# Hybrid decoder layer on one core: token rows scaled, halved and turned by transposing DMAs instead of loaded turned and scaled by a spread product

## The reference, cut to what matters

```python
h = rmsnorm(x, norm_g)                     # x / sqrt(mean(x^2) + 1e-6) * norm_g, per token
proj = h @ w_in                            # 1024 -> 3072
# stick-breaking attention (8 heads), RG-LRU, cross-attention into 256 memory tokens,
# each times silu of its gate
out = x + concat(sb_out, lru_out, xa_out) @ w_out
```

## Time and profile before

| | |
|---|---|
| median of three runs | 1594.46 us |
| profiled execution | 1595.76 us |
| its span | 1594.0 us |
| granted TensorE clock, mean | 0.99 of full |
| TensorE busy | 1530.7 us |
| VectorE busy | 1066.6 us |
| ScalarE busy | 882.1 us |
| POOL busy | 313.2 us |
| DMA, mean | 126 GB/s |

### The profile page before, as it was taken

The page is one execution under the profiler, slowest core; times in us unless marked ns, Lnnn a source line. Parts: engine busy times, 40 slices in busy tenths (PEclk is TensorE's granted clock), DMA queues, the critical chain, the costliest instruction groups (busy, mean ns, idle before and its releaser), DMA issues.

```text
span 1594.0 us, 29935 instructions
## 1 busy us (share of the span) xinstructions
PE 1530.7 (96%) x10886; PEld 748.6 (47%) x10886; DVE 1066.6 (67%) x1932; ACT 882.1 (55%) x1593; POOL 313.2 (20%) x305
## 2 busy tenths in 40 slices
PE   4889999999999999999999999999999999999976
PEld 1344444444444444444444444444444444444432
DVE  5889666676666667666666666666766666676662
ACT  5887455565445556544556644555654455565450
POOL 2122111222211222221222221112222112221100
PEclk9999999999999999999999999999999999999987
DMA  9355554544545454554545454544445454545443
GB/s 366 142 155 117 131 125 108 125 121 120 135 102 139 105 128 109 128 132 109 121 122 123 109 130 120 123 111 122 120 119 133 103 140 102 128 112 126 113 90 93
DMA packets 368711, 201.62 MB, mean 126 GB/s; under 512 B 333792, under 2 KB 334240, under 8 KB 367520
## 3 DMA queue, kind: packets, MB, share of 16 engines
q1 hardware_dynamic: 368384, 200.98, 49.4%
q10 hardware_dynamic: 288, 0.13, 0.0%
HBM read 70.73 MB, written 50.53 MB: 76 GB/s over the span
## 4 chain that ended last, share of the span: by engine, by line
PE 69%; ACT 14%; issue 6%; DVE 3%; SPq 0%; DMA 0%; ACTq 0%; POOL 0%; POOLq 0%; DVEq 0%
PE bank L1654 21%; PE bank L1656 21%; PE bank L1655 21%; ACT fail_and_take L936 2%; PE bank L1698 2%; ACT L929 1%; ACT spare L957 1%; ACT L947 1%; ACT L971 1%; ACT L975 1%; PE bank L1799 1%; ACT fail_and_take L826 1%; PE bank L1820 1%; PE bank L1707 1%; DVE spare L1448 1%
## 5 line engine op out<-in xcount | busy, mean ns | idle before, releaser
L1654 PE MATMUL bank<-w_pair,x_hi 128*128 128x512 f16 x1536 | 584.4, 380 | 12.0 <-DVE w_pair L1119 4.8
L1655 PE MATMUL bank<-w_pair,x_hi 128*128 128x512 f16 x1536 | 583.6, 380 | 0.0
L1656 PE MATMUL bank<-w_pair,x_lo 128*128 128x512 f16 x1536 | 583.2, 380 | 0.0
L1654 PEld LDWEIGHTS bank<-w_pair,x_hi 128*128 128x128 f16 x1536 | 150.4, 98 | 188.5 <-issue 11.8
L1656 PEld LDWEIGHTS bank<-w_pair,x_lo 128*128 128x128 f16 x1536 | 150.6, 98 | 182.2 <-issue 1.7
L1655 PEld LDWEIGHTS bank<-w_pair,x_hi 128*128 128x128 f16 x1536 | 150.6, 98 | 165.8 <-issue 1.4
L1012 ACT ACTIVATE spare<-xy,columns 128x1024 f16<-128x1024 f32 x32 | 36.7, 1148 | 340.5 <-DVE columns L1514 340.5
L1654 PE MATMUL bank<-wo_pair,y_hi 128*128 128x512 f16 x512 | 196.1, 383 | 8.3 <-DMA y_lo<-spare 8.2
L1655 PE MATMUL bank<-wo_pair,y_hi 128*128 128x512 f16 x512 | 196.1, 383 | 0.0
L1656 PE MATMUL bank<-wo_pair,y_lo 128*128 128x512 f16 x512 | 195.8, 382 | 0.0
L651 POOL TENSOR_TENSOR fail_and_take<-fail_and_take,seen 128x512 f32<-128x512 f32 x32 | 42.7, 1336 | 694.9 <-ACT fail_and_take L803 694.9
(11 more groups left out here) (247 smaller groups left out, 2414.6 us busy)
## 6 DMA issues: line engine op xcount, KB each, us to landing
xy<-in_x SPq DMA_DIRECT2D x32, 512.0 KB, 3.4
x_t<-in_x_turned SPq DMA_DIRECT2D x32, 512.0 KB, 4.7
spare<-in_x SPq DMA_DIRECT2D x32, 512.0 KB, 4.2
out<-spare SPq DMA_DIRECT2D x32, 512.0 KB, 2.6
gate_kept<-gate SPq DMA_DIRECT2D x32, 256.0 KB, 2.2
v_kept<-v_sb SPq DMA_DIRECT2D x32, 256.0 KB, 2.1
fail_and_take<-v_sb SPq DMA_DIRECT2D x64, 128.0 KB, 2.3
q_kept<-q_t SPq DMA_DIRECT2D x32, 256.0 KB, 4.0
```

The source lines that it names most:

```text
L1654: pe.matmul(dst, hi[:, k, :], pair[:, 0, k, :], start=k == 0, stop=False)
L1655: pe.matmul(dst, hi[:, k, :], pair[:, 1, k, :], start=False, stop=False)
L1656: last = pe.matmul(dst, lo[:, k, :], pair[:, 0, k, :], start=False, stop=k == KD - 1)
```

## The change

For tile 0 nothing changes. From tile 1 on, the turned load, the diagonal, the spreading product and the scaling are gone. ScalarE multiplies `xy` by the token's factor into a high half, row by row (`x_halves[:, 0]`, laid over `x_t32`), VectorE makes the low half from the same, and SP turns both into `x_hi` and `x_lo` by a transposing DMA each (`turn_rows`), after the last input product of tile n. `project(0)` waits for both landings. In step 0 `turn_rows` stands ahead of the turns of q, k and xq; in later steps behind the store of the gate and the turns of the probabilities, ahead of the store of v. In step 1 the probabilities are turned early, so there it stands right behind the store of the gate. The second part of the w_out load moves behind step 0's turns. In step 0 and 1 the casts move to other places in ScalarE's and VectorE's order. The diff, cut to its core:

```diff
-        rs_diag = spare[:, 2 * D + LW:2 * D + LW + P]
+        x_halves = x_t32[:, :, :].rearrange("p k t -> p (k t)").bitcast(F16).rearrange("p (a c) -> p a c", a=2)
@@ SP
-            def load_out_chunks():
+            def load_out_chunk_6():
                 sp.wait_ge(w_lo, highs(4))
                 sp.dma_start(staged_out(6, slice(0, KD)), w_out_g[0]).then_inc(stage_loaded[1], 16)
+
+            def load_out_chunk_7():
                 sp.dma_start(staged_out(7, slice(0, 6)), w_out_g[1][:, 0:6, :]).then_inc(stage_loaded[3], 16)
                 sp.wait_ge(m_kv, MT)
                 sp.dma_start(staged_out(7, slice(6, KD)), w_out_g[1][:, 6:KD, :]).then_inc(stage_loaded[3], 16)
...
                 if isinstance(n, int) and n == 1:
-                    have(sp, s["x_sq"], n)
+                    have(sp, s["x_lo_done"], n)
                     sp.dma_start(xy[:, :], x_t[n + 1]).then_inc(x_loaded, 16)
...
-                    have(sp, s["x_lo_done"], n)
-                    sp.dma_start(x_t32[:, :, :], x_turned[n + 1]).then_inc(xt_loaded, 16)
...
-                    load_out_chunks()
+                    load_out_chunk_6()
...
+                def turn_rows():
+
+                    have(sp, proj_done[5], n)
+                    have(sp, s["x_hi_done"], n + 1)
+                    turn(x_hi[:, :, :], x_halves[:, 0, :], rows_turned)
+                    have(sp, s["x_lo_done"], n + 1)
+                    turn(x_lo[:, :, :], x_halves[:, 1, :], rows_turned)
+
+                if isinstance(n, int) and n == 0:
+                    turn_rows()
                 if A:
...
+                if isinstance(n, int) and n == 0:
+                    load_out_chunk_7()
                 if A:
                     have_dma(sp, kept["gate"], n - 1)
                     keep("gate", gate_kept, gate[:, p, 0:GC], n, [s["gate_sb"]])
                 if B and not early:
                     probs_turned()
+                if A and X and not (isinstance(n, int) and n == 0):
+                    turn_rows()
                 if A:
                     have_dma(sp, kept["v"], n - 1)
@@ POOL
-                    have(pool, s["x_diag"], n)
+                    have(pool, s["x_lo_done"], n)
@@ ScalarE
                 def rows_high():
 
-                    have(act, s["x_scaled"], n + 1)
-                    if A:
-                        have(act, proj_done[5], n)
-                    act.activation(x_hi[:, :, :], x_t32[:, :, :], ACT.Copy).then_inc(s["x_hi_done"], 1)
+                    if isinstance(n, int) and n < 0:
+                        have(act, s["x_scaled"], n + 1)
+                        act.activation(x_hi[:, :, :], x_t32[:, :, :], ACT.Copy).then_inc(s["x_hi_done"], 1)
+                    else:
+                        have(act, s["x_rs"], n + 1)
+                        have(act, s["x_lo_done"], n)
+                        have_turned(act, rows_turned, n - 1)
+                        act.activation(x_halves[:, 0, :], xy[:, :], ACT.Copy, scale=rs_x[:, :]).then_inc(s["x_hi_done"], 1)
...
@@ VectorE
+                def rows_low():
+                    have(dve, s["x_hi_done"], n + 1)
+                    if isinstance(n, int) and n < 0:
+                        dve.tensor_tensor(x_lo[:, :, :], x_t32[:, :, :], x_hi[:, :, :], ALU.subtract
+                                          ).then_inc(s["x_lo_done"], 1)
+                    else:
+                        dve.scalar_tensor_tensor(x_halves[:, 1, :], xy[:, :], rs_x[:, :], x_halves[:, 0, :],
+                                                 ALU.mult, ALU.subtract).then_inc(s["x_lo_done"], 1)
...
                     if X:
-                        have(dve, s["x_sq"], n + 1)
+                        have(dve, s["x_lo_done"], n + 1)
...
@@ TensorE
                 if A:
-                    have(pe, s["x_hi_done"], n)
-                    have(pe, s["x_lo_done"], n)
+                    if static and n == 0:
+                        have(pe, s["x_lo_done"], n)
+                    else:
+                        have_turned(pe, rows_turned, n - 1)
                 project(0, [(s["gate_sb"], n - 1), (s["out0_read"], n - 3)])
...
-                if X and not (static and n in (0, 1)):
+                if static and n < 0:
                     spread_rows()
```

More of the change, by code:

```diff
@@ L261, in hybrid_layer @@
         xt_loaded = sem("xt_loaded")
+        rows_turned = sem("rows_turned")
         res_loaded = sem("res_loaded")
@@ L327, in halves_of_heads @@
             return qk[:, 0:GC], qk[:, GC:2 * GC], xq
-        def diagonal_of(tile):
-            return tanh_l[:, 0, :] if isinstance(tile, int) and tile < 2 else rs_diag
         def have_turned(eng, signal, tile):
@@ L431, in _ @@
             sp.dma_start(xy[:, :], x_t[0]).then_inc(x_loaded, 16)
-            sp.dma_start(x_t32[:, :, :], x_turned[0]).then_inc(xt_loaded, 16)
+            sp.dma_start(x_t32[:, :, :], x_turned).then_inc(xt_loaded, 16)
             sp.dma_start(given[:, :], per_partition).then_inc(const_loaded, 16)
@@ L818, in row_squares @@
                     if early:
-                        have(act, s["x_diag"], n)
+                        have(act, s["x_rs"], n)
                         act.wait_ge(w_sum, 6 + OUT_SUMS)
@@ L866, in body @@
                     chunk_sum(3)
+                    rows_high()
                     chunk_high(2)
@@ L963, in body @@
                     heads_high()
+                if early:
+                    rows_high()
                 if first:
@@ L999, in body @@
                     memory_values(1)
-                if X and not first:
+                if X and not (first or early):
                     rows_high()
@@ L1232, in row_diagonal @@
                         dve.wait_ge(ident_moved, 32)
-                    dve.tensor_scalar(diagonal_of(n + 1), ident[:, :], rs_x[:, :], None, ALU.mult).then_inc(s["x_diag"], 1)
+                    dve.tensor_scalar(tanh_l[:, 0, :], ident[:, :], rs_x[:, :], None, ALU.mult).then_inc(s["x_diag"], 1)
                 if first:
@@ L1345, in body @@
                 if first:
-                    scale_rows()
+                    rows_low()
                 if A:
@@ L1365, in silu_stick @@
                     silu(s["sg_read"], s["gate_sb"], PROJ[0][:, :], slice(0, GC), G_SG)
-                def rows_low():
-                    have(dve, s["x_hi_done"], n + 1)
-                    dve.tensor_tensor(x_lo[:, :, :], x_t32[:, :, :], x_hi[:, :, :], ALU.subtract
-                                      ).then_inc(s["x_lo_done"], 1)
                 def values_low():
@@ L1400, in body @@
                     out_rows_top()
-                    row_diagonal()
                 if third:
@@ L1411, in body @@
                 if first:
-                    rows_low()
                     values_low()
@@ L1450, in body @@
                     last.then_inc(s["h_done"], 1)
-                if X and not (first or early):
+                if isinstance(n, int) and n < 0:
                     row_diagonal()
@@ L1464, in body @@
                     stick(0)
-                if early:
-                    rows_low()
                 if A and not first:
                     values_low()
+                if isinstance(n, int) and n < 0:
+                    scale_rows()
                 if X and not (first or early):
-                    scale_rows()
                     rows_low()
@@ L1704, in spread_rows @@
                     have(pe, s["x_diag"], n + 1)
-                    if B:
-                        have(pe, s["gates_read"], n - 1)
-                    pe.matmul(SMALL[:, 0:P], ones[:, :], diagonal_of(n + 1), start=True, stop=True).then_inc(s["x_wide"], 1)
+                    pe.matmul(SMALL[:, 0:P], ones[:, :], tanh_l[:, 0, :], start=True, stop=True).then_inc(s["x_wide"], 1)
                 def out_first():
@@ L1733, in values_product @@
                         pe.wait_ge(mv_made, 2)
-                    if X:
-                        have(pe, s["x_scaled"], n + 1)
                     if last_one:
@@ L1903, in laid_out @@
         "x": i["x"],
-        "x_turned": x.reshape(-1, P, x.shape[1] // P, P).transpose(0, 3, 2, 1),
+        "x_turned": x[:128].reshape(P, x.shape[1] // P, P).transpose(2, 1, 0),
         "mem": i["mem"],
```

4 lines of the change are left out of this document (removed).

## The result

The changed kernel takes 1597.42 us, the median of 20 runs (1593.23 to 1601.80), against 1594.53 us for 20 runs of the kernel before (1592.78 to 1596.42): a ratio of 1.0016, 95% interval 1.0008 to 1.0023, so the change loses 1.3 to 3.7 us, clear of the noise. The forecast was 1595.2, a loss of 0.7.

A forecast was written before the change was run, and what follows sets the result against it. A steady tile was taken to cost TensorE's work plus holes, the first three and last two tiles being bound by chains. Sum: -13.7 + 0.6 + 13.8 = +0.7 us, giving 1595.2 us, range 1592 to 1598.

The forecast's parts named there:

- The two long waits for x_lo: Sign of being right: TensorE waits about 5.5 us near 85 and 9 to 10 us before tile 2, clock halved after each.
- lower bound of 9: Low bound, in us, on the first tiles' loss of 13.8, meant for no fall of the clock.
- The steady gain, 13.7 us: Tiles 3 to 30: without the spreading product, output products start sooner, saving 0.54 and 0.46 us in turn; 13.7 in all.
- the wait in tile 4: Loop's first tile: its turns come later, so TensorE waits 0.3 us; likewise in tile 30, 0.6 together.
- The slack of half a microsecond: Steady tile: x_lo lands at 738.65, the next tile's first product comes at 739.15, so no wait.
- Transposing against plain transfers: Landings of 256 KB: turned 3.1 to 3.4 us, plain 2.1, against the skill's rule that both are equally fast.
- Tile 1, +2.9: Before tile 1: x_hi's first issue takes 1.99 us, x_lo lands at 87.8, so the tile starts 2.9 us later.
- The clock behind it: After the wait before tile 1, TensorE at half clock adds 1.7 us.
- Step 1's start, +3.6: SP's queue in tile 1: 2.9 + 1.7 us later, less 1.0 absorbed by ScalarE's wait for xy.
- dearer start: Rival: more half clock, or the w_out load holds xy back and ScalarE starts 2 to 4 us later; 1600, chance 0.16.
- Tile 2, +7.6 from SP's queue: Before tile 2: SP's full queue delays both turns until after the gate store, landing at 134.0, 7.6 us late.
- Half clock behind tile 2, 2.2, and x_res, 0.4: Half clock adds 2.2 us; tile 2's 2.4 us stall goes, but tile 3 waits for x_res, issued late, +0.4.

The follow-up runs named there:

- e2: Changed kernel, with the diagonal and spreading product made again in each step from 2 on, result unread; 1609.36 us.
- e3: Changed kernel, with one extra turn of the high half into unused columns in each step from 2 on, ahead of the needed two; 1631.36 us.
- e4: Changed kernel, with 10 and 38 unread TensorE products in the waits ahead of tiles 1 and 2; 1596.78 us.
- e6: Changed kernel, with the load of tile 2's rows issued ahead of the second part of the output weights; 1597.71 us.
- e9: As e7, but only tiles 0 and 1 are loaded the old way instead of the first three; 1592.43 us.
- e5: Changed kernel, with tile 2's turns issued right behind those of the high halves of queries and keys; 1594.34 us.
- e10: As e9, with tile 2's turns issued right behind those of the high halves of queries and keys; 1589.30 us.
- e11: The changed kernel measured and profiled once more, unchanged; 1595.85 us, ratio 1.0014 to the kernel before.
- e1: Changed kernel, with tiles 0 to 2 done as in the kernel before and the change only from tile 3 on; 1586.39 us.
- e7: As e1, with the load of tile 0's rows for the sum issued ahead of keeping and copying tile 2's values in step 2; 1583.98 us.

## Why the prediction was right, step by step

The time was 2.2 us above the forecast and inside its own range of 1592 to 1598, near the upper end; a small loss from two halves that nearly cancel is what happened. Some of the nearness is luck: in the first three tiles the terms missed by +1.4, +0.5 and -1.3, and their sum came out at 14.3 us against 13.8. The two long waits for x_lo came where they were put, 4.8 and 8.6 us where 5.5 and 9 to 10 were. (The lower bound of 9 was loose: the terms without the clock's add up to 9.9.)

- *The steady gain, 13.7 us.* Right in size and cause. The hole is 0.21; the period fell by 0.50 (46.85 to 46.35), and e2 gave it back by restoring only the product, its diagonal and its waits. With the wait in tile 4 the 28 tiles gave 12.8, forecast 13.1.
- *The slack of half a microsecond.* Measured 0.6: x_hi issued 1.34 ahead of x_lo, landing 3.1 against 3.15. e3 shows what lies behind it. At the ends of steps 4 and 30 I put 0.3 each; step 4 had 0.66 and step 30 none.
- *Transposing against plain transfers.* The rows hold for the new turns too: 3.1 to 3.4 us from issue to landing for 256 KB, and 2.1 for the plain store of v, of the same size. The Trainium skill (Advanced Engine Details and Errata, X-Bar Transpose) puts transposing DMAs on trn2 level with regular ones; for transfers of this size the trace does not agree, and the measurement decides. The comparison needs care, which the prediction did not take: the plain stores of q and k, 256 KB too, take 4.0 and 4.4 us in the kernel before, but they are issued right behind a 512 KB load. With no other transfer in flight at its issue a turn (y_hi, at 745.00 in the kernel before) took 3.25 us.
- *Tile 1, +2.9.* It was 2.0: the first transposing issue took 1.35, not the 1.99 of the earlier trace rows. In e4 it did take 2.13, and tile 1 started at 88.38, 3.5 later. I took for a property of the run's first turn what is not one. All thirteen profiles have exactly one long issue (1.8 to 2.3 us) in step 0, and it is the first turn issued while TensorE has products running: q_t at 85.56 before, the fifth turn at 87.53 in the changed kernel, whose first four fall into TensorE's wait, and x_hi at 82.83 in e4, where the extra products run. Why is not shown. The clock behind it cost what I put: in the 6.5 us from 84.5 TensorE issued 10 products at half clock, against 30 before; from its start at 86.89, 24 products took 2.1 us longer than before (7.47 against 5.40; 1.7 put).
- *Step 1's start, +3.6.* It was 5.0, the term that was too small. I let ScalarE's wait for xy absorb 1.0, but the weights' load ahead of xy made that landing 4.7 late instead. That was my rival "dearer start", by its second mechanism; e6 shows that without it 0.75 comes back (with a tile 1 that began 0.5 later in its profile), the rest being tile 1's own lateness.
- *Tile 2, +7.6 from SP's queue.* It was 8.1 (16.8 us from the probabilities' turns to tile 2, against 8.7), and e9 has it at 8.7, with a start that was 2.6 us late instead of 5.0. Counted in the same way, e5 took 4.6 and e10 4.9 of it away by reordering the queue alone. The prediction put all of it down to the full queue; some 1.1 us are the longer chain (e10).
- *Half clock behind tile 2, 2.2, and x_res, 0.4.* From tile 2 to tile 3 it was 1.3 together: the clock cost 1.4 in the first 24 products, the stall at the spread shrank by 1.0 and not by the whole 2.1, since the output product now waits 1.06 in its place, the product itself (0.5) went, and the wait ahead of tile 3 grew by 1.6 instead of 0.4. Step 2's saved stall went straight into that wait, which I had said only for the load's issue.
- *What moved the median by the last 2 us.* The sum was made for one profiled execution. The kernel before has no wait over 2.6 us on TensorE between 47 and 1500 us; the changed one has three (4.8, 8.6 and 3.4 us, ahead of tiles 1, 2 and 3), and where and for how long half clock follows differs between its two profiles. The forecast had this as a fixed term. That this lifts the median is read from the mean clocks (0.980 to 0.989 in these 20 runs, 0.988 to 0.993 in those of the kernel before beside the experiments), not shown by an experiment: e4, made to test it, did not bring the time down.

What stays open: why the same wait costs the clock in one execution and not in the next. The runs show only that it does. Ahead of tile 3 the waits were 3.25 us in e5 and 3.26 in e6, and the 24 products behind them took 9.2 us; they were 3.29 in e11, 3.35 in e9 and 3.37 in the changed kernel, and the 24 products took 6.3.

## What to carry to other kernels

A step that is moved to a queue can cost nothing in a steady loop and a good deal at the edges: here SP had room in every steady tile, but in the two tiles in which TensorE waits for the first results its queue was in the way, and over 4 us of issue and landing stood bare. Where a loop's first iterations are written out anyway, keep the old way there: that turned a change of +0.2% into one of -0.6% (e1), or -0.7% with tile 0's rows sooner (e7). And before a new DMA goes on a queue, read the slack to the next product in the trace: here 0.6 us, and one transfer more cost 34 us.

The Trainium skill (DMA: Bandwidth & Descriptors, Silent corruption: two transposing streams in flight at once) says that transposes issued from SP and from ScalarE can corrupt each other when they are in flight together, unless the later one waits until the earlier one has completed. So ScalarE's queue could relieve SP only behind such waits; no run here tried it.

## What the runs showed of the hardware

- SP issues a transposing DMA in 1.2 to 1.35 us, but now and then one takes 2.0 to 2.6: q_t at 125.50 (2.12) in the changed kernel and at 123.04 (2.56) in e9. In step 0 it was in all thirteen profiles the first turn issued while TensorE had products running, whichever turn that was (85.56, 1.99 before; 87.53, 2.02 changed; 82.83, 2.13 in e4). In the start such an issue can stand on the path.
- A third turn of 256 KB in a row cost SP 1.57 us on average (1.68 in step 17), not its 1.24 of issue (e3).
- A wait of 8.6 us halved TensorE's clock over the wait and the 3 us of products behind it, and busy work in the wait kept it at 1.00 (e4). Waits of 3 to 4 us did so in one execution (e1, 0.50 after 3.58 us; e4, after 3.99) and not in others (e7, after 2.93; the changed kernel, 1.00 after 3.37 at tile 3), and the length doesn't decide it: 0.51 after 3.25 in e5.
- Moving a load forward on SP's queue by 1.9 us made it land only 0.64 sooner (e7: 4.64 us to landing, 3.39 in e1). Three transfers of v are issued right behind it there; that they are the reason is likely, not shown.
- From issue to landing a turn of 256 KB took 3.25 us with no other transfer in flight at its issue (y_hi, 745.00, kernel before), a plain store of 256 KB 2.1 (v) and, behind a 512 KB load, 4.0 (q).
